# A two-layer diffusion trunk on 8 cores: first heads prepared in the projection, values two steps behind the scores, PSUM banks apart, 14 adaLN pieces moved into the feed-forward

## The chip, the cores and the metric

The program runs on all 8 cores of one Trainium2 chip (cores 0 to 3 are one die, 4 to 7 the other). Each core computes one share of the requests on its own, with no traffic between cores, and all of them read the same weights. The metric is the device time of the slowest core in microseconds. The engines of a core are TensorE (PE), ScalarE (ACT), VectorE (DVE), GpSimd (POOL) and SyncE (SP); POOL and SP also issue the DMAs.

## The reference, cut to what matters

```python
for i in range(2):                       # layer 0: pooling + latent attention, layer 1: gated MLP
    sh1, sc1, g1, sh2, sc2, g2 = split(silu(cond) @ ada_w[i] + ada_b[i], 6)      # adaLN, 6 x 1024
    h = rms_norm(x, norm_mix_g[i]) * (1 + sc1) + sh1
    if i == 0:
        z = h @ ab_w_in                  # u (512) | cq (384) | ckv (256) | krope (32)
        y_pool = (windowed_mean(u, w in (2, 4, 8, 16)) - u) @ w_pool * scale
        q = rope(rms_norm(rms_norm(cq) @ w_uq))          # 8 heads of 96
        k, v = rms_norm([rms_norm(ckv) @ w_ukv, krope]), ...   # 512 cached keys in front
        y = concat(y_pool, softmax(q k / sqrt(96)) v) @ ab_w_out
    else:
        y = chunk_gmlp(h)                # u * (W_s v + b), chunks of 128
    x = x + g1 * y
    h = rms_norm(x, norm_ffn_g[i]) * (1 + sc2) + sh2
    x = x + g2 * ((silu(h @ ffn_wg) * (h @ ffn_wu)) @ ffn_wd)          # D_FF 2816
```

Each core has 512 context tokens (2 sequences of 256) and 1024 latent tokens, which attend to 512 cached and the 1024 latent keys. Matmuls are bf16 with f32 sums.

## The kernel before, in words

The 1536 tokens are three blocks of 512 (block 0 is context). The residual `xb` stays in SBUF with features on the partitions. A helper class records every operation, so most instructions have the line of a helper (L230 is `mm`, L228 `mm` with a group check off, L239 a transpose, L247 an activation, L251, L259, L268 and L274 element-wise operations, L220 a DMA). Program order on each engine is the order in which the Python generators are stepped: a main generator yields, and fillers (other generators) are stepped between its pieces. The helper also makes every engine wait where two engines touch the same PSUM bank.

**Weights** come through one list (`ents`) in a fixed order, by one `Stream` of 11 slots of 512 KB (bf16; the f32 source is 1 MB). A slot's next DMA is issued on POOL's queue when `W.done` frees it. Slots 8, 9 and 10 are given up after their first use. All 48 adaLN pieces (`ada_piece`: 16 matmuls of 2 columns into one bank, then a small DVE addition into `mod`) come before the output projection's weights: 8 at the start, the others during the preparation of pair 0 and the attention.

**Stages of layer 0**, in order of time:

- `Norm.gen` squares a block (ACT, POOL), sums it on PE with a matrix of ones, and writes the normalised block `hy[b]`. Block 0 and the first 8 adaLN pieces go first.
- `inproj(b)` for b = 0, 1, 2: ten steps of 8 matmuls (kv, q, u and rotary parts), their norms and evacuations, in banks 0 to 5. While block b runs, the norm of block b + 1 is stepped (`weave_in`, by an account of estimated idle time), and with b = 1 also `pooling` of block 0. Block 2 has no filler.
- `qkv(0)` prepares keys, queries and values of the first pair of heads: 14 units (6 q, 4 k, 4 v), with smaller steps that are called one or more units later (`later`, `tick`): `reduce`, `rnorm`, `rotate`, `turn` (8 transposes), `sums`. Pooling of blocks 1 and 2 and some adaLN pieces are stepped beside it. Each pooling tile is made by narrow matmuls against `band`, evacuated by ACT (`pbf`), multiplied by `pool_w`, and evacuated again by ACT.
- `attention`: 4 pairs of heads, 28 steps each (4 context steps, 24 of one 128-key tile against 1024 queries). A step is `score` (2 matmuls of 512 columns into one of the two double banks `SD`, then one exp on ACT into `pt`), then `values` of the step before (8 matmuls of 65 columns, into banks 4 and 5). Between them `qkv` of the next pair, the adaLN pieces and `spread` (4 transposes) are stepped. All of these share banks 6 and 7 (`FB`) in turn.
- Output projection, then the feed-forward `ffn(0)`: groups of 3, 3, 3 and 2 weight pieces; `up` is 16 matmuls of 512 columns, `down` 6 (the last groups 10). Layer 1 follows (`gmlp`, `ffn(1)`).

The changed places are in `build`: the slots and `ents`, `ffn`, the code from `cached_keys` to the output projection.

Of the kernel before, what the change touches and what calls it, by code (L numbers as in the profile page):

```python
# [363 lines left out]
def build():  # L364
# [42 lines left out]
    with ExitStack() as es:  # L407
# [16 lines left out]
        slots = [new("wslot%d" % i, [128, 2048], BF16, high=(i >= 8)) for i in range(11)]  # L424
# [31 lines left out]
        ent_ada(8, 48)  # L456
# [31 lines left out]
        W.retire.update((8, 9, 10))  # L488
# [150 lines left out]
        def ffn(l, need):  # L639
# [37 lines left out]
            for gi in range(1, 4):  # L677
                for j in range(2 * (FGRP[gi][1] - FGRP[gi][0])):
# [3 lines left out]
                    if j % 2 == 1:  # L682
                        up_done(FGRP[gi][0] + j // 2)
# [144 lines left out]

        def inproj(b):
# [43 lines left out]
            if b == 0:  # L873
# [4 lines left out]
                held.append(ckvf)  # L878
            pq.append(proj(5, W.get("in_q1"), 0))
# [30 lines left out]
        FB = (6, 7)  # L910

        def pooling(blocks, banks, step, evac):

            for b in blocks:
                seqs = [(0, 2), (2, 4)] if b == 0 else [(4, 12)]
                for g in range(4):
# [22 lines left out]
                    evac(pbf[:], ps[:], 1.0 / w)  # L939
# [31 lines left out]
        for b in range(3):  # L971
            drain(norms[b])
            fill = collections.deque()
            if b < 2:
                fill.append(norms[b + 1])
            if b > 0:
                fill.append(pooling([b - 1] if b == 1 else [], (6,), 1.3, lambda o, i, sc: P.ts("dve", o, i, sc, None, ALU.mult)))
            weave_in(inproj(b), fill)
        for key in ("in_kv", "in_q0", "in_q1", "in_u0", "in_u1"):
            W.done(key)  # L980
        N.close()
        drop(*sqb.t, *rsb.t, *t2k.t, sqkr, ropek, *held)

        wukv = W.get("ukv")
        wuq = [W.get("uq0")[:, 0, :], W.get("uq0")[:, 1, :], W.get("uq1")[:, 0, :]]
        ptr = Ring([new("pt%d" % i, [128, 1024], BF16) for i in range(3)])
        rdr = Ring([new("rd%d" % i, [128, 4], F32) for i in range(2)])

# [6 lines left out]
        kvq = [new_kvq(0)]  # L995
        qfr = Ring([new("qf%d" % i, [128, 4, 96], F32) for i in range(5)])
        qsr = Ring([new("qs%d" % i, [128, 4, 96], F32) for i in range(2)])
        qtr = Ring([new("qt%d" % i, [128, 4, 96], BF16) for i in range(6)])
        qrr = Ring([new("qr%d" % i, [128, 2, 4, 32], F32) for i in range(2)])
        sqk = Ring([new("sqk%d" % i, [128, 512], BF16) for i in range(2)])  # L1000
        ssr = Ring([new("ss%d" % i, [128, 8], F32) for i in range(4)])

        def qkv(p, banks):
# [3 lines left out]
            for hl in range(2):  # L1007
                P.dma("sp", kT[64:96, hl, :], kro[64:96, :], "kro%d" % (p % 2))
# [16 lines left out]
            def turn(b, qts):  # L1025
                ps = P.bank(banks).bitcast(BF16)
# [28 lines left out]
            def q_unit(b, u):  # L1055
# [3 lines left out]
                ps = P.bank(banks)  # L1059
# [7 lines left out]
                P.cp("dve", qf[:].rearrange("p a d -> p (a d)"), ps[:, 0:384])  # L1067
# [10 lines left out]
            def sums(kb, sq):  # L1078
                ps = P.bank(banks)
# [5 lines left out]
            def k_unit(kb):  # L1085
                ps = P.bank(banks)
# [7 lines left out]
            def v_unit(kb):  # L1094
                ps = P.bank(banks)
# [3 lines left out]
                P.cp("dve", V[:, kb * 4:kb * 4 + 4, :, 0:64], ps[:].rearrange("p (t h d) -> p t h d", t=4, h=2))  # L1099
# [7 lines left out]
            order = [("q", b, u) for b in range(3) for u in range(2)] + [(c, kb) for kb in (3, 0, 1, 2) for c in "kv"] if p == 0 else [("q", 0, 0), ("k", 3), ("q", 0, 1), ("v", 3), ("q", 1, 0), ("k", 0), ("q", 1, 1), ("v", 0),  # L1107
# [28 lines left out]
        def spread(p, ytok, b):  # L1136
            ps = P.bank(FB).bitcast(BF16)
# [260 lines left out]
```

How the kernel before makes its waits and increments, by code:

```python
    def op(self, e, fn, reads, writes, inc=True):  # L181
        rr = [x for x in (self.reg(a) for a in reads) if x is not None]
        wr = [x for x in (self.reg(a) for a in writes) if x is not None]
        waits = self._waits(e, self._deps(rr, wr, e))
        eng = self.E[e]
        attach = (e != "pe")
        for s, v in (waits[:-1] if attach else waits):
            eng.wait_ge(self.sem[s], v)
        ins = fn(eng)
        if waits and attach:
            ins._wait_ge(self.sem[waits[-1][0]], waits[-1][1])
        if inc:
            ins.then_inc(self.sem["c_" + e], 1)
            self.cnt[e] += 1
            ev = ("c_" + e, self.cnt[e])
        else:
            ev = ("c_" + e, self.cnt[e] + 1)
        self._record(rr, wr, ev)
        self.nins += 1
        return ins
# [1 line left out]
    def dma(self, q, out, in_, key, slow=False):  # L202
        rr = [x for x in (self.reg(in_),) if x is not None]
        wr = [x for x in (self.reg(out),) if x is not None]
        waits = self._waits(q, self._deps(rr, wr))
        eng = self.E[q]
        for s, v in waits:
            eng.wait_ge(self.sem[s], v)
        k = self.dsem(key)
        side = out if wr else in_
        nm = side.tensor.name
        last = self.dlast.get(k)
        if last is not None and last != nm and self.known[q].get(k, 0) < self.dtot[k]:
            eng.wait_ge(self.sem[k], self.dtot[k])
            self.known[q][k] = self.dtot[k]
        self.dlast[k] = nm
        if slow:
```

## Time and profile before

| | us |
|---|---|
| median of 3 runs (lowest, highest) | 1257.72 (1257.38, 1264.88) |
| profiled execution, its own time | 1258.27 |
| span of its slowest core, core 2 | 1257.2 |
| spans of the 8 cores | 1245.5 to 1257.2 |
| PE, DVE, ACT, POOL busy | 1130.3, 478.0, 428.9, 226.9 |

### The profile page before, as it was taken

How to read it: one execution, taken by the hardware profiler on the slowest of the kernel's cores; microseconds unless marked ns; L12 is line 12 of the kernel's file. 1: busy time of each engine (PE TensorE's matmuls, PEld its weight loads, DVE VectorE, ACT ScalarE, POOL GpSimd, SP SyncE). 2: the span in 40 equal slices, each digit the busy share in tenths (PEclk: the TensorE clock that was granted, in tenths of full speed). 3: DMA queues.
4: the chain of work that ended last, by engine and by line, in shares of the span. 5: the costliest groups of instructions: out<-in, count | busy, mean ns of one | idle time of the engine just before them, and what ended most of it. 6: DMA issues, size and time to landing. Idle time of an engine off the chain costs nothing.

```text
span 1257.2 us, 17850 instructions; the slowest of 8 cores (1245.5 to 1257.2 us)
## 1 busy us (share of the span) xinstructions
PE 1130.3 (90%) x6857; PEld 547.4 (44%) x6857; DVE 478.0 (38%) x814; ACT 428.9 (34%) x669; POOL 226.9 (18%) x347
## 2 busy tenths in 40 slices
PE   2447877887899999999999999998899999999998
PEld 1223455555443444444444444443344444444443
DVE  0335445555136311151251263565522215125133
ACT  2435457777735511101101156543541110110100
POOL 4311245335113100000000022234310000000000
PEclk9988879899699999999999999998899999999999
DMA  9980245775991434215225206004534421400013
GB/s 189 229 152 1 43 73 93 127 130 100 162 168 21 64 56 78 34 34 84 34 34 84 51 1 109 1 1 63 92 48 68 67 36 32 84 17 1 1 78 124
DMA packets 24977, 90.04 MB, mean 72 GB/s; under 512 B 3392, under 2 KB 3776, under 8 KB 24128
## 3 DMA queue, kind: packets, MB, share of 16 engines
q0 software_dynamic: 21312, 77.10, 36.7%
q1 hardware_dynamic: 3584, 11.80, 2.8%
q8 instruction: 58, 0.95, 0.3%
q14 instruction: 23, 0.19, 0.1%
HBM read 153.85 MB, written 6.88 MB: 128 GB/s over the span
## 4 chain that ended last, share of the span: by engine, by line
PE 76%; DMA 6%; DVE 5%; ACT 5%; issue 4%; POOL 3%; POOLq 0%; ACTq 0%; DVEq 0%
PE pb L230 74%; DMA band<-band 3%; ACT pt L247 3%; DMA wslot<-ada_w 3%; PE pb L228 2%; DVE xtmp L268 1%; DVE kT L274 1%; POOL wslot L220 1%; PE pb L239 1%; POOL qs L251 1%; DVE xb L268 0%; POOL xtmp L251 0%; ACT hy L247 0%; POOL xsq L251 0%; DVE ytk L251 0%
## 5 line engine op out<-in xcount | busy, mean ns | idle before, releaser
L230 PE MATMUL pb<-hb,wslotx 128*128 128x512 bf16 x1200 | 264.5, 379 | 0.0
L230 PE MATMUL pb<-hb,wslot 128*128 128x512 bf16 x1104 | 247.8, 384 | 0.0
L247 ACT ACTIVATE sg<-pb 128x512 f32<-128x512 f32 x132 | 78.7, 596 | 472.7 <-PE pb L230 472.7
L251 DVE TENSOR_TENSOR apart<-pb,sg 128x512 bf16<-128x512 f32 x132 | 91.3, 692 | 369.1 <-PE pb L230 346.2
L268 DVE SCALAR_TENSOR_TENSOR xb<-pb,mod,xb 128x512 f32<-128x512 f32 x192 | 143.7, 749 | 146.1 <-PE pb L230 146.1
L230 PEld LDWEIGHTS pb<-hb,wslotx 128*128 128x128 bf16 x1200 | 117.4, 98 | 141.6
L230 PEld LDWEIGHTS pb<-hb,wslot 128*128 128x128 bf16 x1104 | 109.0, 99 | 133.3 <-issue 6.0
L230 PE MATMUL pb<-apart,wslot 128*128 128x512 bf16 x768 | 167.1, 379 | 0.0
L247 ACT ACTIVATE pt<-pb,rk 128x1024 bf16<-128x1024 f32 (+1 forms) x128 | 117.8, 952 | 42.3 <-PE pb L230 41.4
L230 PEld LDWEIGHTS pb<-apart,wslot 128*128 128x128 bf16 x768 | 75.2, 98 | 90.2
L230 PE MATMUL pb<-hy,wslot 128*128 128x512 bf16 (+1 forms) x336 | 84.5, 404 | 6.6 <-ACT hy L247 4.5
L230 PE MATMUL pb<-qT,kT 96*128 96x512 bf16 (+1 forms) x224 | 73.8, 417 | 0.0
L268 DVE SCALAR_TENSOR_TENSOR xtmp<-xb,AA,xrs 128x512 f32<-128x512 f32 x72 | 62.5, 906 | 9.8 <-ACT xrs L247 9.4
L247 ACT ACTIVATE xsq<-xb 128x512 bf16<-128x512 f32 x72 | 41.9, 622 | 67.6 <-PE pb L230 36.3
L230 PE MATMUL pb<-apart,wslotx 128*128 128x512 bf16 x288 | 62.5, 379 | 0.0
L228 PEld LDWEIGHTS pb<-V,pt 128*128 128x128 bf16 x768 | 36.1, 103 | 56.9 <-issue 49.7
L230 PE MATMUL pb<-xsq,ones 128*128 128x512 bf16 x96 | 30.2, 409 | 31.3 <-ACT xsq L247 23.7
L228 PE MATMUL pb<-V,pt 128*128 128x65 bf16 x768 | 43.4, 203 | 16.1 <-ACT pt L247 15.0
L230 PEld LDWEIGHTS pb<-hy,wslot 128*128 128x128 bf16 (+1 forms) x336 | 34.1, 103 | 52.2 <-issue 19.2
L251 POOL TENSOR_TENSOR xtmp<-xb,xrs 128x512 f32<-128x512 f32 x24 | 33.7, 1403 | 117.6 <-ACT hb L247 86.4
L247 ACT ACTIVATE hb<-xtmp,mod 128x512 bf16<-128x512 f32 x54 | 37.6, 720 | 33.5 <-DVE xtmp L268 33.5
L230 PE MATMUL pb<-uTb,wslot 128*128 128x512 bf16 x192 | 47.4, 401 | 0.0
(131 smaller groups left out, 936.2 us busy)
## 6 DMA issues: line engine op xcount, KB each, us to landing
wslot<-ada_w POOLq DMA_DIRECT2D x48, 512.0 KB, 7.3
wslot<-ffn_wd POOLq DMA_DIRECT2D x16, 512.0 KB, 10.4
wslot<-ffn_wu POOLq DMA_DIRECT2D x12, 512.0 KB, 7.8
wslotx<-ffn_wg POOLq DMA_DIRECT2D x12, 512.0 KB, 16.9
y<-xb SPq DMA_DIRECT2D x12, 512.0 KB, 2.6
wslot<-ffn_wg POOLq DMA_DIRECT2D x10, 512.0 KB, 7.4
wslotx<-ffn_wu POOLq DMA_DIRECT2D x10, 512.0 KB, 15.4
xb<-x_in POOLq DMA_DIRECT2D x4, 1024.0 KB, 44.5
```

The source lines that it names most:

```text
L220: ins = eng.dma_start(out=out, in_=in_)
L228: return self.op("pe", lambda g: g.matmul(out, lhsT, rhs, start=start, stop=stop, skip_group_check=True), [lhsT, rhs], [out], inc=inc)
L230: return self.op("pe", lambda g: g.matmul(out, lhsT, rhs, start=start, stop=stop), [lhsT, rhs], [out], inc=inc)
L239: return self.op("pe", lambda g: g.transpose(out, in_, ident), [in_, ident], [out])
L247: return self.op("act", lambda g: g.activation(out=out, in_=in_, func=func, bias=bias, scale=scale), reads, [out])
L251: return self.op(e, lambda g: g.tensor_tensor(out=out, in0=in0, in1=in1, op=op), [in0, in1], [out])
L268: return self.op(e, lambda g: g.scalar_tensor_tensor(out=out, in0=in0, scalar=sc, in1=in1, op0=op0, op1=op1), reads, [out])
L274: return self.op(e, lambda g: g.tensor_copy(out=out, in_=in_), [in_], [out])
```

## The change

1. The stream has 10 slots in place of 11, and slots 7, 8 and 9 are given up after their first use; an eighth slot (`wsloty`) comes back at the start of attention, and 8 in place of 7 behind it.
2. 14 adaLN pieces (34 to 47) leave the list before the output projection and stand among the weights of `ffn(0)`, two behind each of the up pieces 3 to 9. Each pair is computed when the up piece is done. `ensure_AA` of layer 1's second norm moves behind `ffn(0)`.
3. The cached keys' squares (`cached_keys`) move from ahead of `inproj(0)` into it.
4. `together` steps the fillers of `inproj` evenly: all of the norm of block 1 in block 0, all of the norm of block 2 with pooling of block 0 in block 1, and 12 steps of `qkv(0)` in block 2, in banks 6 and 7. The order of units of `qkv(0)` is new, and its q and v evacuations go to ACT. The rest of `qkv(0)` then runs beside pooling of blocks 1 and 2, whose evacuations alternate between ACT and DVE and whose product comes one tile later, with four banks each.
5. In attention `values` runs two steps behind `score`. The large tiles of `qkv` have bank 6 alone; its small tiles, `spread` and the adaLN pieces have bank 7 alone.
6. The rotary keys are copied into each of the two key buffers once, not once for each pair.

```diff
-        slots = [new("wslot%d" % i, [128, 2048], BF16, high=(i >= 8)) for i in range(11)]
+        slots = [new("wslot%d" % i, [128, 2048], BF16, high=(i >= 7)) for i in range(10)]
...
                     ent(("wu", l, k), ffn_wu[l, k], 8, 256)
+                    if l == 0 and 3 <= k < 10:
+                        ent_ada(34 + 2 * (k - 3), 36 + 2 * (k - 3))
...
-        ent_ada(8, 48)
+        ent_ada(8, 34)
...
-                        up_done(FGRP[gi][0] + j // 2)
+                        k = FGRP[gi][0] + j // 2
+                        up_done(k)
+                        if l == 0 and 3 <= k < 10:
+                            for _ in range(2):
+                                ada_piece(pool=B7)
...
-                    evac(hy[b][:, g, :], ps2[:], vecs[:, 128 + g:129 + g])
-                    yield step
+                    late.append((b, g, pbf))
+                    if len(late) > lag:
+                        product(*late.popleft())
+                        yield step
...
+        drain(norms[0])
+        together(inproj(0), 10, [(norms[1], 26)])
+        drain(norms[1])
+        pool0 = pooling([0], (6,), 1.3, (on_dve, on_dve))
+        together(inproj(1), 10, [(norms[2], 36), (pool0, 9)])
...
+        bk0 = [FB]
+        q0 = qkv(0, bk0, bk0)
+        together(inproj(2), 10, [(q0, 12)])
...
-                    if pend is not None:
-                        for b in values(*pend):
-                            todo.append((i + 2, functools.partial(spread, pend[0], pend[3], b)))
+                    if len(pend) == 2:
+                        sums(pend.popleft())
...
-                    pend = (p, step, pt, ytok)
+                    pend.append((p, step, pt, ytok))
...
-        together(qkv(0, (0, 1, 2, 3, 4, 5)), 18, [(pool12, 18), (ada, 6)])
+        together(pooling([1, 2], (4, 5, 6, 7), 0.5, (in_turn, in_turn), 1), 16, [(q0, 9)])
+        drain(q0)
...
-            nxt[0] = qkv(p + 1, FB) if p < 3 else iter(())
+            nxt[0] = qkv(p + 1, [(6,)], [SB]) if p < 3 else iter(())
```

**POOL's queue ahead of `band`.** Before (`cckv` and `band` are inputs of the cached values and of pooling; `w_ukv`, `w_uq` and `ada_w` are weights):

```order
L220 DMA wslot_16_58<-w_ukv 128x2048
L220 DMA wslot_17_59<-w_uq 128x1536
L220 DMA wslot_18_60<-w_uq 128x768
L220 DMA wslot_19_61<-ada_w 128x2048
L220 DMA wslot_20_62<-ada_w 128x2048
L220 DMA wslot_21_63<-ada_w 128x2048
L251 TENSOR_TENSOR xtmp_48_123<-xb_1_43,xrs_46_121 128x512
L251 TENSOR_TENSOR xtmp_49_124<-xb_1_43,xrs_46_121 128x512
L220 DMA ckvn_35_99<-cckv 128x1024
L220 DMA band_89<-band 128x1728
```

Now:

```order
L220 DMA wslot_17_59<-w_ukv 128x2048
L220 DMA wslot_18_60<-w_uq 128x1536
L220 DMA wslot_19_61<-w_uq 128x768
L220 DMA wslot_20_62<-ada_w 128x2048
L251 TENSOR_TENSOR xtmp_47_121<-xb_1_43,xrs_45_119 128x512
L251 TENSOR_TENSOR xtmp_48_122<-xb_1_43,xrs_45_119 128x512
L220 DMA ckvn_34_97<-cckv 128x1024
L220 DMA band_87<-band 128x1728
```

One adaLN piece stands ahead of `band` where three stood; the rest of the list ahead of it has the same bytes.

**PE in the second block of the attention's first pair.** Before (`qT,kT` is a score, `V,pt` the values, `cqn` a q unit, `ckvn` on the left a k unit):

```order
L230 MATMUL pb<-qT_82_1005,kT_81_1004 128x512 x2
L228 MATMUL pb<-V_83_1006,pt_76_999 128x65 x8
L230 MATMUL pb<-qT_82_1005,kT_81_1004 128x512 x2
L228 MATMUL pb<-V_83_1006,pt_77_1000 128x65 x8
L230 MATMUL pb<-ckvn_32_96,wslot_16_58 128x512 x2
L230 MATMUL pb<-scT_55,wslot_21_63 128x2 x16
L230 MATMUL pb<-qT_82_1005,kT_81_1004 128x512 x2
L228 MATMUL pb<-V_83_1006,pt_78_1001 128x65 x8
L230 MATMUL pb<-wslot_17_59,cqn_95 128x192 x2
```

Now:

```order
L230 MATMUL pb<-qT_72_849,kT_71_848 128x512 x2
L228 MATMUL pb<-V_73_850,pt_101_1219 128x65 x8
L230 MATMUL pb<-ckvn_31_94,wslot_17_59 128x512 x2
L230 MATMUL pb<-qT_72_849,kT_71_848 128x512 x2
L228 MATMUL pb<-V_73_850,pt_102_1220 128x65 x8
L230 MATMUL pb<-wslot_18_60,cqn_93 128x192 x2
```

The rows of a step look alike; the `pt` that the values read is now that of two scores earlier. The q unit behind a k unit still comes one step later, and here the k unit has no adaLN piece behind it.

**PE at the start of `inproj(2)`.** Before:

```order
L230 MATMUL pb<-hy_40_104,wslot_22_64 128x512 x16
L230 MATMUL pb<-hy_40_104,wslot_23_65 128x512 x8
L230 MATMUL pb<-sqb_53_128,ones_47 128x512
L230 MATMUL pb<-sqb_54_129,ones_47 128x512
L230 MATMUL pb<-hy_40_104,wslot_23_65 128x512 x8
```

Now:

```order
L230 MATMUL pb<-hy_39_102,wslot_22_64 128x512 x8
L230 MATMUL pb<-wslot_18_60,cqn_93 128x192 x2
L230 MATMUL pb<-wslot_19_61,cqn_93 128x192
L230 MATMUL pb<-wslot_18_60,cqn_93 128x192 x2
L230 MATMUL pb<-wslot_19_61,cqn_93 128x192
L230 MATMUL pb<-hy_39_102,wslot_22_64 128x512 x8
L230 MATMUL pb<-wslot_18_60,cqn_93 128x192 x2
L230 MATMUL pb<-wslot_19_61,cqn_93 128x192
```

The groups of 8 now have units of `qkv(0)` between them. In `ffn(0)` two runs of 16 two-column matmuls (`scT`) stand behind the sixth up tile pair of each piece, with nothing else moved there.

## Rows read from the trace of the kernel before

**Rows 1.** Spans and clock: the slowest core and the fastest.

```profile
core 2: 1257.2 us, clock 0.955
core 4: 1245.5 us, clock 0.971
```

**Rows 2.** Busy time by stretch: stretch, length, each engine busy (instructions), clock, DMA.

```profile
core 2: us, PE busy (x) PEld busy (x) DVE busy (x) ACT busy (x) POOL busy (x), PEclk, DMA share, GB/s
79.00:90.00 11.00, 0.56 (x6) 0.59 (x7) 0.04 (x1) 0.00 (x0) 0.00 (x0) 0.65 0.93 140
90.00:123.00 33.00, 26.76 (x129) 11.33 (x126) 20.29 (x43) 17.72 (x29) 4.05 (x3) 0.86 0.00 0
123.00:144.00 21.00, 20.47 (x102) 9.49 (x102) 7.22 (x11) 8.91 (x16) 0.92 (x2) 0.91 0.00 1
144.00:180.00 36.00, 22.57 (x267) 17.46 (x266) 18.29 (x49) 16.93 (x34) 17.47 (x36) 0.73 0.49 89
180.00:226.00 46.00, 38.54 (x520) 25.62 (x521) 23.14 (x55) 33.19 (x45) 19.38 (x39) 0.83 0.57 92
226.00:272.00 46.00, 38.16 (x570) 25.60 (x571) 26.44 (x66) 34.47 (x48) 19.85 (x40) 0.93 0.67 118
272.00:317.00 45.00, 35.27 (x547) 24.10 (x544) 24.82 (x59) 32.28 (x42) 20.57 (x41) 0.96 0.68 118
317.00:354.00 37.00, 32.10 (x370) 17.11 (x368) 5.66 (x23) 28.82 (x30) 7.39 (x14) 0.72 1.03 162
500.00:600.00 100.00, 100.00 (x465) 45.36 (x464) 31.85 (x44) 11.94 (x20) 4.75 (x9) 1.00 0.30 50
```

**Rows 3.** Timeline, 36 to 90 us: start, duration, instruction, idle before it.

```profile
36.46 0.56 PE L230 MATMUL pb<-scT,wslot 128*128 128x2 bf16 x16 [3.02 <-DMA wslot<-ada_w]
39.64 0.51 PEld L230 LDWEIGHTS pb<-scT,wslot 128*128 128x128 bf16 x16 [2.70 <-issue]
39.67 0.56 PE L230 MATMUL pb<-scT,wslot 128*128 128x2 bf16 x16 [2.65 <-DMA wslot<-ada_w]
47.62 0.54 POOL L220 DMA_DIRECT2D band<-band  x1
89.44 1.02 PE L228 MATMUL pb<-band,utok 128*128 128x129 bf16 x8 [12.22 <-DMA band<-band]
90.25 3.06 PE L230 MATMUL pb<-hy,wslot 128*128 128x512 bf16 x8
93.36 1.89 PE L230 MATMUL pb<-hy,wslot 128*128 128x512 bf16 x8
```

**Rows 4.** PE's timeline, 116 to 126 us: the first groups of block 2.

```profile
117.68 1.91 PE L230 MATMUL pb<-hy,wslot 128*128 128x512 bf16 x3 [3.29 <-ACT hy L247]
120.23 2.42 PE L230 MATMUL pb<-hy,wslot 128*128 128x512 bf16 x4 [0.63 <-ACT hy L247]
123.22 3.14 PE L230 MATMUL pb<-hy,wslot 128*128 128x512 bf16 x7 [0.58 <-ACT hy L247]
```

**Rows 5.** What PE waited for, 145 to 190 us: total, times, longest.

```profile
PE pb L230 <- DVE pbf L251: 4.8, 3, 1.8
PE pb L239 <- POOL qt L251: 4.2, 3, 2.5
PE pb L230 <- DVE mod L251: 2.4, 2, 1.7
```

**Rows 6.** What PE waited for, 190 to 352 us.

```profile
PE pb L228 <- ACT pt L247: 14.0, 35, 0.7
PE pb L230 <- DVE kT L274: 5.7, 8, 1.1
```

**Rows 7.** Groups of PE, 190 to 352 us: busy, mean ns, idle before.

```profile
L230 PE MATMUL pb<-scT,wslot 128*128 128x2 bf16 x528 | 18.6, 164 | 5.1 <-DVE kT L274 2.1 <-DVE qT L259 0.9 <-DVE V L274 0.8
```

**Rows 8.** Timeline around one k unit, 228 to 236 us.

```profile
229.87 1.06 PE L230 MATMUL pb<-ckvn,wslot 128*128 128x512 bf16 x2
230.96 0.60 ACT L247 ACTIVATE sqk<-pb 128x512 bf16<-128x512 f32 x1 [0.60 <-PE pb L230]
231.59 1.41 DVE L274 CAST kT<-pb 64x512 bf16<-64x512 f32 x2 [0.48 <-PE pb L230]
```

**Rows 9.** ACT's timeline in the last pair, 329 to 354 us.

```profile
330.96 1.11 ACT L247 ACTIVATE pt<-pb,rk 128x1024 bf16<-128x1024 f32 x1 [0.61 <-PE pb L230]
335.48 1.11 ACT L247 ACTIVATE pt<-pb,rk 128x1024 bf16<-128x1024 f32 x1 [0.61 <-PE pb L230]
342.02 10.98 ACT L247 ACTIVATE pt<-pb,rk 128x1024 bf16<-128x1024 f32 x10 [0.40 <-PE pb L230]
```

More of the change, by code:

```diff
@@ L878, in inproj @@
                 held.append(ckvf)
+            if b == 2:
+                W.done("in_kv")
+                W.done("in_q0")
             pq.append(proj(5, W.get("in_q1"), 0))
@@ L910, in build, with pooling, product @@
         FB = (6, 7)
-        def pooling(blocks, banks, step, evac):
+        SB = (7,)
+        def pooling(blocks, banks, step, evac, lag=0):
+            late = collections.deque()
+            def product(b, g, pbf):
+                ps2 = P.bank(banks)
+                P.mm(ps2[:], pw[:, g, :], pbf[:])
+                evac[1](hy[b][:, g, :], ps2[:], vecs[:, 128 + g:129 + g])
             for b in blocks:
@@ L954, in pooling @@
                     drop(*[utok.pop(t) for t in range(4, 12)])
+            while late:
+                product(*late.popleft())
+                yield step
         pbr = Ring([new("pbf%d" % i, [128, 512], BF16) for i in range(2)])
@@ L969, in weave_in @@
                     debt = 0.0
[L971 to L987, printed above, removed]
         def new_kvq(i):
@@ L993, in new_kvq, with rotary_keys, qkv @@
             return d
[L995 to L1003, printed above, removed]
+        def rotary_keys(p):
+            for hl in range(2):
+                P.dma("sp", kvq[p % 2]["kT"][64:96, hl, :], kro[64:96, :], "kro%d" % (p % 2))
+        def qkv(p, banks, small):
             d = kvq[p % 2]
             kT, qT, V, rk = d["kT"], d["qT"], d["V"], d["rk"]
-            for hl in range(2):
-                P.dma("sp", kT[64:96, hl, :], kro[64:96, :], "kro%d" % (p % 2))
+            if p == 1:
+                rotary_keys(p)
             lag = collections.deque()
@@ L1025, in turn @@
             def turn(b, qts):
-                ps = P.bank(banks).bitcast(BF16)
+                ps = P.bank(small[0]).bitcast(BF16)
                 for hl in range(2):
@@ L1058, in q_unit @@
                 ss, sr, qts = qst[b]
-                ps = P.bank(banks)
+                ps = P.bank(banks[0])
                 for i in range(2):
@@ L1078, in sums @@
             def sums(kb, sq):
-                ps = P.bank(banks)
+                ps = P.bank(small[0])
                 for i in range(4):
@@ L1085, in k_unit @@
             def k_unit(kb):
-                ps = P.bank(banks)
+                ps = P.bank(banks[0])
                 P.mmg(ps[:], [(wukv[:, kc, p * 256:p * 256 + 128], ckvn[kb][:, kc, :]) for kc in range(2)])
@@ L1094, in v_unit @@
             def v_unit(kb):
-                ps = P.bank(banks)
+                ps = P.bank(banks[0])
                 for i in range(4):
@@ L1187, in attention, with sums @@
             steps = [("ctx", hl, s) for hl in range(2) for s in range(2)] + [("lat", hl, n) for hl in range(2) for n in range(12)]
-            pend = None
+            pend = collections.deque()
             i = 0
             todo = collections.deque()
+            def sums(w):
+                for b in values(*w):
+                    todo.append((i + 2, functools.partial(spread, w[0], w[3], b)))
             for p in range(4):
@@ L1228, in before @@
             drain(nxt[0])
-            nxt[0] = qkv(p + 1, FB) if p < 3 else iter(())
-        left = 50 - ada_state["done"]
+            nxt[0] = qkv(p + 1, [(6,)], [SB]) if p < 3 else iter(())
+        left = 36 - ada_state["done"]
         for i, _ in enumerate(attention(before)):
@@ L1244, in build @@
             drop(*r.t)
-        drop(cqn, *ckvn, kro, krs, band, icnt, pw, ropeq, gqr)
+        drop(cqn, *ckvn, kro, krs, ropeq, gqr)
         hbs = [new("hb%d" % i, [128, 8, 512], BF16) for i in range(3)]
         N = Norm()
-        W.more([new("wslotx%d" % i, [128, 2048], BF16) for i in range(7)])
+        W.more([new("wslotx%d" % i, [128, 2048], BF16) for i in range(8)])
         norms = {}
```

92 lines of the change are left out of this document (61 added, 31 removed).

## The prediction, made before the changed kernel had run

> **What bounds the kernel now.** I read the table by stretch first. PE is fully busy through the feed-forward [rows 2], in its row of 500 to 600 us, so what is added there is paid in full, and what can be won lies ahead of 354 us, where PE idles. Then the timeline for the first stall: PE stands still for 12.22 us until `band` has landed, with POOL, ACT and DVE idle too [rows 2, 3]. Next the start of block 2, where PE waits 3.29, 0.63 and 0.58 us for normalised tiles [rows 4]. From 144 to 180 us, the preparation of pair 0, PE is busy 22.57 of 36 us at a clock of 0.73 [rows 2], and the waits name evacuations and rotations one by one [rows 5]: a chain of latencies, no full engine. In attention, 180 to 354 us, PE is busy 144.1 us and ACT 128.8 us of 174 [rows 2]; PE's largest wait is for the exps, 14.0 us in 35 pieces, then for the key copies, 5.7 us [rows 6].
>
> **The start and block 1.** PE's last two adaLN pieces of the start came 3.21 us apart (36.46 to 39.67), each after a wait for its DMA [rows 3]: that is the price of a piece on the full queue. Two fewer stand ahead of `band`, so it lands 6.4 us earlier, near 83. The bounds are 0 (another transfer is last) and 12.2 (the whole wait goes). Behind the stall, 8 matmuls take 3.06 us where the next 8 take 1.89 [rows 3]: 1.2 us of low clock, mostly gone with a wait of two or three us. One more projection group (1.9) and three sums of squares (3 x 0.2) now stand ahead of `band` and fill what is left of the wait: 2.5 us. With the norm of block 2 stepped evenly, it is done inside block 1, and the 4.5 us of rows 4 go. Sum 14.6. Against it: ACT and DVE are busy 17.7 and 20.3 of 33 us there [rows 2], and the norm's squares now stand in ACT's queue ahead of the projection's own; I charge 2.6 us. **Term: -12 us** (-4 to -16). Moving the cached keys costs nothing: ACT's 0.6 us and DVE's small work fall beside 8 matmuls.
>
> **Block 2 and pair 0.** From 123 to 178 us, 55 us, PE is busy 20.5 + 22.6 us [rows 2]. Of the latter, five adaLN pieces (5 x 0.56, the duration in rows 3) leave and the first scores (1 us) belong to attention; 18.7 us stay, at a clock of 0.73. If half of the low clock's time comes back, that is some 15.5, so PE's work is 36. Block 2 had 8.9 us of ACT and 7.2 of DVE in 21 [rows 2]; it can take half of `qkv(0)` and become 26 to 27 us long. The other half beside pooling has 16 evacuations of pooling, 8 each on ACT and DVE, and no longer waits for each one's product (4.8 us in rows 5), but the last rotation chain of POOL (4.2 us in rows 5) still ends before the last transposes. I put stalls at 5 us: 41 in place of 55. **Term: -14 us.** Bounds: -18 (almost no stall) and -5 (half the stall stays and the clock stays low).
>
> **Attention.** The values of a step now wait for an exp that is one step older, so the 14 us in 35 pieces [rows 6] go, and about 1 us of the same ahead of 190. The score two steps on waits for the same exp (its double bank), so no wait of the other kind is lost or gained. Nine adaLN pieces fewer (26 in place of 35), at 0.56 us: -5.0; the same price, 18.6 us for 33 pieces, stands in [rows 7]. Against it: a k unit holds its bank from the matmuls' start at 229.87 to the end of the key copies at 233.0, 3.1 us [rows 8], and with bank 6 alone the next large tile waits for all of it. By the calls (18 in 25 steps) two of four k units in a pair have the next tile one step, some 1.4 us, behind them: 6 x 1.4 = 8.4 us where 5.7 stood, +2.7. Small tiles collide in bank 7 in turn, transposes (an evacuation of 0.8 us) ahead of an adaLN piece above all, as they did in two banks. The last pair will be bound by the exps: the last ten came 1.10 us apart (10.98 us) [rows 9], so 24 of them and four context steps make some 30 us where 37 are now; 5 of these 7 us are waits counted above, so a further gain is left out. To be careful I leave +2 us for exps that PE now has to wait for where ACT is behind. 14 + 1 + 5 - 2.7 - 2 = 15.3. **Term: -15 us.** Bounds: -33 (the low clock in 180 to 354, 0.83, 0.93, 0.96 and 0.72 in rows 2, goes as well) and +3 (every k unit stalls PE and the exps' wait moves to the scores).
>
> **Feed-forward.** 14 pieces of 0.56 us on a full PE: **+7.8 us.** The 16 weight loads of a piece took 0.51 us [rows 3], so they lie within the 0.56. The Trainium skill ("TensorE: Matmul & The Clock Gate", LDWEIGHTS) gives a load as its columns divided by 1.2 GHz, 107 ns for 128, which would make a piece 1.7 us, the term 24 and the total 1241; the row is at 32 ns, between the two figures of its section on weight-path modes for a fast load (32 cycles, and half of 107 ns). The DMAs are hidden: the queue's share is 0.30 there [rows 2], and each pair of pieces stands far ahead of its use. The rotary copies left out and the slots cost nothing: SP has little else, and the output projection's stretch waits for no weight.
>
> **Sum**, against the profiled execution's own 1258.27, which is 0.5 us above the median: -12 - 14 - 15 + 7.8 = -33. **Predicted 1225 us.**
>
> **The rivals.**
>
> *The wait is exchanged.* The exps' wait ends, but scores, k units in bank 6 and small tiles in bank 7 take its place: the k unit's 3.1 us against a step of 1.5 speaks for it, that PE and ACT are both under 83% busy speaks against. Attention gains only its five us for the pieces: 1225 + 10 = 1235, and with less gained in block 2, 1240. Chance 0.24, with the case that the values' lag does nothing, because PE already queues behind the score's own wait.
>
> *The clock comes back.* In rows 2 the clock is 0.73 to 0.96 from 90 to 354 us; the slowest core has 0.955 over the span, the fastest 0.971, and the two differ by 11.7 us [rows 1]. If fewer stalls hold PE at 2.4 GHz, the last pair alone gains 4 to 5 us: steps there take 4.52 us for three (330.96 to 335.48), where the last ten took 1.10 each [rows 9]. With as much in the pairs before and in 144 to 180: 1225 - 15 = 1210. For it: idle time falls. Against it: PE did little in the steps at low clock that it won't do again. The same page of the Trainium skill (The HAM clock gate) says that activity releases the throttle and idling restores it, which is this rival; the rows agree after the 12 us wait. Chance 0.18.
>
> *The feed-forward starves.* The 14 pieces share slots and queue with its weights, and stand ahead of the down weights in a list that keeps its order. If the queue were full there, each would cost its 3.2 us: 14 x 3.2 = 45, and 1225 + 45 = 1270, slower than before. It decides only from a share near 1; the row has 0.30, and 45 us over the 200 us of pieces 3 to 9 add 0.22. Chance 0.05.
>
> *The preparation doesn't fit into block 2* (ACT's queue holds back the projection's squares, POOL's chain ends as late as before): term -5 and block 1's -4 give 1225 + 17 = 1242. Chance 0.08.
>
> **How the numbers follow.** The forecast has 0.45, with 1215 to 1236 as its own range. For 8 in 10 the range takes in the clock's case and the exchanged wait: 1203 to 1244. This kernel's time can be told apart within about 1%, 12.6 us. Faster than 1245 are the forecast, the clock, most of the exchanged wait and most of the last case: 0.84; within 1%: 0.10; slower by over 1%: 0.06.
>
> **What would show it.** `band`'s wait under 4 us and its matmuls near 83 us; no wait for `hy` at block 2's start; the first score near 152 us; PE's wait for `pt` under 3 us and that for `kT` near 8; attention some 161 us long where it is 176; 14 runs of `scT` in the feed-forward at 0.56 us each, with no DMA wait. I am wrong if attention is as long as now with another name in its wait list, or if the first score comes after 165 us.

## The result, and the profile after

The changed kernel takes 1240.77 us (median of 3 runs, 1240.61 to 1241.51) where the kernel before takes 1257.72: a ratio of 0.9858, 95% interval 0.9808 to 0.9907. It is 17 us faster, where 33 had been forecast. Executions in which one die was granted a lower clock throughout are left out of every ratio in this document. 1240.8 lies inside the range of 1203 to 1244, but outside the forecast's own 1215 to 1236, and next to the rival "the wait is exchanged" (1235 to 1240).

The spans of all cores fell. The slowest is now core 6; core 4, the fastest before [rows 1], fell by 7 us only. Both lines are of the changed kernel's list of cores:

```profile
core 2: 1231.4 us, clock 0.977
core 6: 1240.5 us, clock 0.972
```

Busy time by stretch of core 6 after the change, with the columns of [rows 2], cut at its own stages: block 1 behind `band`, block 2, the rest of pair 0's preparation, the four pairs of attention, the feed-forward.

```profile
83.00:109.00 26.00, 19.77 (x113) 9.29 (x115) 16.79 (x39) 14.90 (x25) 3.58 (x4) 1.00 0.01 1
109.00:135.00 26.00, 23.98 (x157) 12.70 (x156) 13.29 (x26) 15.59 (x31) 6.94 (x13) 1.00 0.00 1
135.00:158.00 23.00, 14.12 (x138) 11.37 (x139) 13.87 (x32) 9.38 (x19) 9.71 (x23) 0.78 0.64 92
158.00:203.00 45.00, 33.73 (x477) 24.30 (x478) 23.38 (x54) 31.69 (x44) 17.42 (x35) 0.92 0.35 61
203.00:252.00 49.00, 38.99 (x500) 28.11 (x504) 24.60 (x59) 32.74 (x45) 18.18 (x37) 0.83 0.44 71
252.00:297.00 45.00, 33.99 (x471) 25.25 (x476) 24.53 (x58) 30.43 (x42) 18.74 (x38) 0.89 0.44 76
297.00:336.00 39.00, 30.23 (x414) 19.49 (x412) 7.45 (x27) 31.02 (x36) 8.99 (x17) 0.93 1.01 161
500.00:600.00 100.00, 99.45 (x541) 46.60 (x548) 32.14 (x50) 11.34 (x19) 7.93 (x15) 1.00 0.49 88
```

Set beside [rows 2], the stretches ahead of attention shrank and those of attention did not: on this core the pairs take 45, 49, 45 and 39 us where they took 46, 46, 45 and 37. PE is busy less in them (137 us against 144), so its idle time grew. The feed-forward's DMA share went from 0.30 to 0.49 with PE at 99% busy.

The start, on PE's timeline (start, duration, instruction, idle before it). It answers to [rows 3]:

```profile
82.12 0.84 PE L230 MATMUL pb<-xsq,ones 128*128 128x512 bf16 x3
82.91 0.61 PE L228 MATMUL pb<-band,utok 128*128 128x129 bf16 x8
83.36 1.89 PE L230 MATMUL pb<-hy,wslot 128*128 128x512 bf16 x8
```

`band`'s matmuls come at 82.91 in place of 89.44 and wait for nothing (on the other cores 0.8 to 3.2 us); the group behind them takes 1.89 us where it took 3.06. Block 2's first matmul starts at 108.94 and the group waits for no tile. Before [rows 4] it started at 117.68 and got its last normalised tile at 123.22, with seven matmuls of block 2 done by then.

What PE waited for between block 2 and the first score, 134 to 158 us (total, times, longest), where [rows 5] stood:

```profile
PE pb L239 <- POOL qt L251: 3.7, 3, 1.8
PE pb L239 <- DVE ksb L251: 3.1, 1, 3.1
PE pb L230 <- ACT hy L247: 1.0, 2, 0.7
PE pb L230 <- DVE pbf L251: 0.8, 1, 0.8
```

And in attention, 158 to 335 us, in answer to [rows 6]:

```profile
PE pb L230 <- DVE kT L274: 11.9, 10, 2.1
PE pb L228 <- DVE rd L1174: 6.6, 4, 2.6
PE pb L230 <- ACT pt L247: 6.0, 20, 0.9
PE pb L239 <- DVE rd L1174: 2.4, 2, 1.7
PE pb L239 <- DVE hy L274: 2.3, 2, 2.1
PE pb L230 <- DVE qT L259: 1.3, 2, 1.0
```

The values no longer wait for exps (L228 on `pt` is down to 0.8 us). The scores now do: by the means over the cores they wait 4.5 us for exps, where they waited for none before. Beside that PE waits for DVE: for key copies, twice as long as before, for the reciprocals (`rd`) that empty the values' banks between two heads, and for small tiles. One k unit, on the timeline of all engines, answers to [rows 8]:

```profile
169.64 0.38 PE L230 MATMUL pb<-ckvn,wslot 128*128 128x512 bf16 x1
170.39 0.59 ACT L247 ACTIVATE sqk<-pb 128x512 bf16<-128x512 f32 x1
171.01 1.41 DVE L274 CAST kT<-pb 64x512 bf16<-64x512 f32 x2 [1.13 <-ACT sqk L247]
172.57 0.66 PE L230 MATMUL pb<-wslot,cqn 128*128 128x192 bf16 x6 [1.87 <-DVE kT L274]
```

The square stands behind an exp on ACT, the two copies behind the square on DVE, and the q unit one step later waits 1.87 us for the bank. Every score behind it in PE's queue waits too. In the last pair ACT sets the pace, as [rows 9] did in its last ten exps: here twelve in 12.58 us.

```profile
320.06 12.58 ACT L247 ACTIVATE pt<-pb,rk 128x1024 bf16<-128x1024 f32 x12 [0.18 <-PE pb L230]
```

To compare kernels I cut each core's PE timeline at three marks (first score, first matmul of the output projection, end) and took means over the 8 cores of the profiled execution. Waits, busy time and granted clock of PE are between the first two marks, in attention; the waits are listed by what they waited for. All waits and the busy time add up to the stretch within 1.2 us:

| kernel | ratio to before | first score at | attention | behind it | waits: pt | kT | rd | all | busy | clock |
|---|---|---|---|---|---|---|---|---|---|---|
| before | 1 | 177.9 | 175.2 | 899.4 | 17.6 | 6.7 | 1.9 | 32.3 | 142.0 | 0.90 |
| after | 0.9858 | 158.3 | 172.7 | 903.8 | 5.6 | 11.2 | 9.1 | 37.4 | 134.9 | 0.90 |
| lag2_only | 0.9980 | 179.5 | 172.1 | 897.9 | 6.6 | 10.9 | 7.6 | 31.4 | 140.2 | 0.88 |
| lag1 | 0.9872 | 160.5 | 173.6 | 904.7 | 19.1 | 9.3 | 1.6 | 38.3 | 134.8 | 0.93 |
| shared | 0.9823 | 159.5 | 167.6 | 903.2 | 5.4 | 9.7 | 8.1 | 32.2 | 135.1 | 0.89 |
| ada_back | 0.9910 | 160.0 | 184.7 | 897.8 | 4.4 | 10.3 | 8.5 | 37.5 | 146.9 | 0.85 |
| slots10 | 0.9968 | 174.2 | 174.5 | 898.3 | 18.5 | 6.7 | 1.9 | 33.9 | 139.9 | 0.91 |
| prep_only | 0.9851 | 160.2 | 174.9 | 897.5 | 17.5 | 5.2 | 1.0 | 28.8 | 144.9 | 0.89 |
| spaced | 0.9715 | 159.8 | 155.6 | 903.4 | 5.7 | 6.4 | 1.4 | 25.5 | 129.6 | 0.92 |
| ada21 | 0.9764 | 159.6 | 160.3 | 906.7 | 6.7 | 7.9 | 8.9 | 30.9 | 129.2 | 0.92 |
| sp_lag1 | 0.9818 | 160.9 | 170.4 | 903.7 | 19.9 | 0.2 | 1.5 | 32.4 | 137.6 | 0.89 |
| sp_bank | 0.9744 | 160.5 | 159.3 | 904.1 | 6.3 | 9.3 | 1.4 | 29.5 | 128.9 | 0.94 |
| sp_eleven | 0.9713 | 159.5 | 156.2 | 903.7 | 5.6 | 6.7 | 1.4 | 25.6 | 130.0 | 0.92 |
| sp_ada21 | 0.9703 | 161.1 | 152.0 | 907.0 | 7.2 | 6.8 | 1.6 | 26.1 | 125.4 | 0.94 |

So the change's 17.8 us of mean span are -19.6 ahead of attention, -2.5 in it and +4.3 behind it.

### The profile page after: what moved, and what is told of

Same layout as the page of the kernel before. It is cut to its first block, busy times and chain, and to the rows that moved or that the text cites. A ratio compares the mean times of both kernels' runs of the same rounds, so it can differ in the third digit from the quotient of the medians.

```text
span 1240.5 us, 17691 instructions; the slowest of 8 cores (1231.4 to 1240.5 us)
## 1 busy us (share of the span) xinstructions
PE 1114.8 (90%) x6753; PEld 552.4 (45%) x6857; DVE 476.9 (38%) x812; ACT 424.0 (34%) x671; POOL 225.4 (18%) x347
## 4 chain that ended last, share of the span: by engine, by line
PE 76%; DVE 7%; ACT 6%; issue 5%; POOL 4%; DMA 3%; DVEq 0%; POOLq 0%; ACTq 0%
PE pb L230 74%; ACT pt L247 3%; DMA wslot<-ada_w 3%; DVE xtmp L268 2%; PE pb L228 1%; DVE kT L274 1%; POOL qr L251 1%; DVE xb L268 1%; ACT hy L247 1%; PE pb L239 1%; POOL wslot L220 1%; POOL qt L251 1%; POOL qs L251 0%; ACT xsq L247 0%; ACT hb L247 0%
## 5 line engine op out<-in xcount | busy, mean ns | idle before, releaser
L230 PE MATMUL pb<-hb,wslot 128*128 128x512 bf16 x1031 | 239.4, 381 | 1.4
L230 PE MATMUL pb<-hb,wslotx 128*128 128x512 bf16 x1037 | 233.8, 379 | 1.1
L230 PEld LDWEIGHTS pb<-hb,wslot 128*128 128x128 bf16 x1056 | 103.5, 98 | 125.1 <-issue 2.3
L230 PEld LDWEIGHTS pb<-hb,wslotx 128*128 128x128 bf16 x1056 | 103.0, 98 | 123.8
L230 PE MATMUL pb<-apart,wslotx 128*128 128x512 bf16 x566 | 135.5, 379 | 0.5
L230 PE MATMUL pb<-apart,wslot 128*128 128x512 bf16 x468 | 114.1, 379 | 0.7
L230 PEld LDWEIGHTS pb<-apart,wslotx 128*128 128x128 bf16 x576 | 56.4, 98 | 67.5
L230 PE MATMUL pb<-hy,wslot 128*128 128x512 bf16 (+1 forms) x281 | 72.8, 405 | 7.5 <-ACT hy L247 4.4
L230 PEld LDWEIGHTS pb<-apart,wslot 128*128 128x128 bf16 x480 | 46.8, 98 | 56.2
L228 PEld LDWEIGHTS pb<-V,pt 128*128 128x128 bf16 x768 | 40.4, 104 | 36.6 <-issue 20.4
L228 PE MATMUL pb<-V,pt 128*128 128x65 bf16 x768 | 44.0, 203 | 8.7 <-DVE rd L1174 6.6
L247 ACT ACTIVATE hb<-xtmp,mod 128x512 bf16<-128x512 f32 x54 | 37.5, 720 | 33.4 <-DVE xtmp L268 33.4
L230 PEld LDWEIGHTS pb<-hy,wslot 128*128 128x128 bf16 (+1 forms) x288 | 29.1, 103 | 44.3 <-issue 17.2
## 6 DMA issues: line engine op xcount, KB each, us to landing
wslot<-ffn_wg POOLq DMA_DIRECT2D x12, 512.0 KB, 11.6
wslotx<-ffn_wg POOLq DMA_DIRECT2D x9, 512.0 KB, 12.5
```

The costliest lines, as they stand in the source:

```text
L228: return self.op("pe", lambda g: g.matmul(out, lhsT, rhs, start=start, stop=stop, skip_group_check=True), [lhsT, rhs], [out], inc=inc)
L230: return self.op("pe", lambda g: g.matmul(out, lhsT, rhs, start=start, stop=stop), [lhsT, rhs], [out], inc=inc)
L247: return self.op("act", lambda g: g.activation(out=out, in_=in_, func=func, bias=bias, scale=scale), reads, [out])
```

## The experiments

The theory after the result: in attention PE takes its work in order, and the waits that it meets on DVE are a queue behind the exps' wait; taking that one away lets PE arrive earlier at the next. The rival is the prediction's sum: each part is worth its price, and some other part lost the rest. Each ratio is to the kernel before, run on the same chip beside it. The twelve kernels fall into three groups, each with a chip of its own: lag2_only, lag1, shared and ada_back; spaced, ada21, slots10 and prep_only; the four named sp_. Between groups a stage can shift without any edit: `band`'s first matmul is at 89.7 us before and at 91.6 in lag2_only, which has the same start.

**lag2_only**: the kernel before with the values two steps behind.

```diff
-                    if pend is not None:
-                        for b in values(*pend):
...
+                    if len(pend) == 2:
+                        sums(pend.popleft())
...
```

> The kernel before, with one part of the change alone: the values run two steps behind the scores. If the prediction's term holds, the 14 to 15 us of waits for exps in attention go and nothing takes their place: 1257.7 - 14 = 1244, with PE's wait for pt under 3 us. If the rival holds (the wait is exchanged), PE now queues at the scores, at the bank of a k unit and at the values' banks behind DVE: 1252 to 1258, with waits for kT, rd and pt at the scores that together grow by 8 us or more.

Measured: 0.9980 (0.9966 to 0.9994), 2.5 us. PE's waits of its slowest core, 190 to 352 us:

```profile
PE pb L230 <- DVE kT L274: 7.6, 7, 2.0
PE pb L228 <- DVE rd L1133: 6.6, 3, 2.3
PE pb L230 <- ACT pt L247: 4.7, 16, 0.5
PE pb L239 <- DVE kT L274: 3.1, 2, 1.9
PE pb L230 <- DMA wslot<-ada_w: 2.9, 3, 1.7
```

By the means, `pt` falls from 17.6 to 6.6 us (the values' part from 17.6 to 0.8, while the scores' part rises from nothing to 5.7), `kT` and `rd` rise by 9.9, and all waits together stay at 31 to 32. That is the exchange, shown with one edit. The prediction's 14 us are refuted for this order of work.

**lag1**: the changed kernel with the values one step behind.

```diff
-                    if len(pend) == 2:
+                    if len(pend) == 1:
```

> The changed kernel with the values one step behind the scores again, everything else kept. Prediction's term: 1240.8 + 14 = 1255. Rival: 1241 to 1246, and PE's waits for kT and rd shrink by about what the wait for pt grows.

Measured: 0.9872 (0.9854 to 0.9891) where the changed kernel has 0.9858. That is 1.8 us, the intervals overlap, and attention is 0.9 us longer by the means. Again `pt` is up by 13.5 and `kT` and `rd` down by 9.4. The prediction's 1255 is out.

**shared**: the changed kernel with banks 6 and 7 in turn for all tiles.

```diff
-        SB = (7,)
+        SB = FB
-            nxt[0] = qkv(p + 1, [(6,)], [SB]) if p < 3 else iter(())
+            nxt[0] = qkv(p + 1, [FB], [FB]) if p < 3 else iter(())
```

> The changed kernel with banks 6 and 7 shared in turn by all tiles of attention again, as before the change. In the changed kernel PE waits 11.9 us for kT where it waited 5.7 before. If bank 6 alone is what doubled it, the wait falls back to about 6 and the time to 1233 to 1236. The prediction's price for the banks was 2.7 us: 1238. If the waits belong to PE's order and not to the banks, the time stays within 1240 to 1242.

Measured: 0.9823 (0.9804 to 0.9842), attention 5.1 us shorter by the means. The two ratios' intervals overlap, but all of the 5.1 us is waits (37.4 to 32.2 in the table), so I take the split to cost 4 to 5 us, more than the 2.7 predicted. What stands behind a wait can't be read from its releaser alone: `kT` fell by 1.5 only, because in shared banks small tiles wait for key copies too. Sorted by what waits, the large tiles (k, q and v units) wait 14.6 us in the changed kernel and 5.6 here, by the means; the small ones (transposes, `spread`, adaLN pieces) 8.8 and 12.0. So the cost is in bank 6, where the prediction had it, and the small tiles lost less with a bank of their own. The q units, changed kernel first, then `shared`, on the slowest core of each (columns as in [rows 7]):

```profile
L230 PE MATMUL pb<-wslot,cqn 128*128 128x192 bf16 x108 | 13.0, 261 | 10.2 <-DVE kT L274 9.2 <-DVE V L274 0.8
L230 PE MATMUL pb<-wslot,cqn 128*128 128x192 bf16 x108 | 13.1, 263 | 4.5 <-DVE kT L274 3.1 <-DVE hy L274 0.6 <-DVE V L274 0.4
```

**ada_back**: the changed kernel with the 14 pieces back in attention.

```diff
-                    if l == 0 and 3 <= k < 10:
-                        ent_ada(34 + 2 * (k - 3), 36 + 2 * (k - 3))
...
-        ent_ada(8, 34)
+        ent_ada(8, 48)
```

> The changed kernel with the 14 adaLN pieces back in attention, none in the feed-forward. The prediction's prices: the feed-forward wins 7.8 us, attention loses 9 to 14 pieces at 0.56: 5 to 8 us, so 1238 to 1241. If attention is held by waits in which the pieces had found cover, it loses under 3 us: 1234 to 1236, and moving them had been a loss.

Measured: 0.9910 (0.9889 to 0.9932). Both expectations had it at 1241 or faster; it is 6 us slower than the changed kernel. The feed-forward wins 6 us, attention loses 12: 0.86 us a piece against 0.43. Moving the pieces paid 6 us, where the prediction's one price of 0.56 us, in either place, made it even. The adaLN pieces' own waits rose from 3.1 to 10.4 us, but all waits together stayed (37.4 and 37.5): the 12 us are busy time, 134.9 to 146.9, of which 14 pieces at 0.40 to 0.56 us explain 6 to 8. The rest goes with a granted clock of 0.85 in place of 0.90.

**slots10**: the kernel before with the new slots alone.

```diff
-        slots = [new("wslot%d" % i, [128, 2048], BF16, high=(i >= 8)) for i in range(11)]
+        slots = [new("wslot%d" % i, [128, 2048], BF16, high=(i >= 7)) for i in range(10)]
...
-        W.retire.update((8, 9, 10))
+        W.retire.update((7, 8, 9))
...
-            if k == 1:
+            if k == 2:
...
+        W.more([new("wsloty", [128, 2048], BF16)])
```

> The kernel before with the stream's 10 slots alone (7 to 9 given up, the eighth back in attention): two adaLN pieces fewer ahead of band. If band alone decides the start of block 1, its first matmul comes 6 us earlier, near 83 us, and the time falls by 5 to 6 us, to 1252. If the time is lost again before attention, because the norm of block 2 isn't ready, it falls by under 2 us.

Measured: 0.9968 (0.9951 to 0.9984), 4 us. `band`'s first matmul comes at 85.2 in place of 89.7 by the means, with a wait of 5.9 us ahead of it in place of 11.7. The line of the slowest core:

```profile
85.57 1.02 PE L228 MATMUL pb<-band,utok 128*128 128x129 bf16 x8 [4.79 <-DMA band<-band]
```

The first score comes 3.7 us earlier: what the queue gives is kept.

**prep_only**: the changed kernel with values one step behind, shared banks and all pieces in attention (the edits of lag1, shared and ada_back together).

> The changed kernel with the values one step behind, banks 6 and 7 shared and all adaLN pieces in attention: what is left is the start, the even stepping and pair 0's preparation in block 2. By the stages measured so far the first score comes 20 us earlier than before the change, and attention carries 5 pieces more than before (34 in place of 35 and 5 outside it, now 40): 1257.7 - 20 + 4 = 1242, 0.987. If attention loses more than that because it starts with less done, 1247 or more.

Measured: 0.9851 (0.9831 to 0.9872), where the whole change has 0.9858. The start and the preparation carry all of the gain that can be told. The three parts that touch attention are worth nothing measurable together, with five more pieces in attention at that.

**spaced**: `shared`, with the 18 calls of the next pair's preparation at chosen steps: a free step behind each k unit, none where a head's values end.

```diff
-            n = i % 28
-            for k in range((n + 1) * 18 // 25 - n * 18 // 25):
-                next(nxt[0], None)
+            if i % 28 in (2, 3, 5, 6, 7, 8, 10, 11, 12, 13, 15, 18, 19, 21, 22, 23, 24, 25):
+                next(nxt[0], None)
```

(The k units fall on steps 3, 8, 13 and 19 of 28, and nothing more is called in 4, 9, 14 and 20.)

> The changed kernel with banks 6 and 7 shared (it measured 0.9823 of the kernel before), and the 18 calls of the next pair's preparation at other steps: behind each k unit a step without a call, and none at the steps where a head's values end. If single long stalls behind a k unit and behind the values' evacuation are what attention loses, PE's waits for kT and rd, 9.7 and 8.1 us, fall by 10 us in sum and the time falls by 6 to 9 us, to 0.976. If waits are only exchanged again (the exps and the low clock bound attention), the wait for pt grows by as much and the time stays at 0.982.

Measured: 0.9715 (0.9691 to 0.9739), 13.6 us below `shared`, with attention at 155.6 us. PE's waits of its slowest core, 159 to 315 us:

```profile
PE pb L230 <- DVE kT L274: 6.6, 9, 0.9
PE pb L239 <- POOL qt L251: 5.9, 3, 2.5
PE pb L230 <- ACT pt L247: 4.4, 17, 0.7
PE pb L230 <- DVE V L274: 1.9, 4, 0.6
PE pb L230 <- DVE rd L1174: 0.9, 3, 0.5
```

In `shared`, on its slowest core from 159 to 327 us, the first two stood so:

```profile
PE pb L228 <- DVE rd L1174: 7.0, 3, 2.6
PE pb L230 <- DVE kT L274: 6.7, 7, 1.6
```

By the means `rd` falls from 8.1 to 1.4, `kT` from 9.7 to 6.4, in pieces of 0.9 us at most where the longest had 1.9, and `pt` grows by 0.3 only; the waits of transposes for POOL's rotations (`qt`) grow from 3.0 to 5.8. The run moves two things at once, and it doesn't separate them: twice as much went from `rd` (no call where a head's values end) as from `kT` (a free step behind a k unit). All waits fell by 6.7 us, of 12.0 us that attention lost; the rest is PE's busy time, 135.1 to 129.6, with the clock up from 0.89 to 0.92.

**sp_lag1**: `spaced` with the values one step behind (the edit of lag1).

> The kernel of the run 'spaced' (0.9715 of the kernel before) with the values one step behind the scores again. With the long DVE stalls gone, the two theories of the lag part: if the lag had been worth nothing because other waits took its place, it should now be worth its 12 us of exp waits, and this run comes out at 0.981. If the lag is worth little in itself, since ACT and PE take turns as the limit, it stays at 0.972 to 0.974.

Measured: 0.9818 (0.9798 to 0.9837). Here the lag is worth 13 us, and attention is 14.8 us longer without it: the size of the prediction's -14, in another schedule. It isn't the prediction's 14 us of waits, though. `pt` is up by 14.2, but all waits by 6.9 only; the other 8.0 us are busy time, 129.6 to 137.6, with the clock down from 0.92 to 0.89. Its slowest core, 159 to 327 us:

```profile
PE pb L228 <- ACT pt L247: 16.4, 34, 1.1
PE pb L228 <- DVE ytk L251: 4.0, 5, 0.8
PE pb L239 <- POOL qt L251: 2.9, 3, 1.7
```

**sp_bank**: `spaced` with the split banks of the change (the edit of shared, undone).

> The kernel of the run 'spaced' with large tiles in bank 6 alone and small ones in bank 7 alone, as in the change. If the split costs because the next large tile comes one step behind a k unit, the free step now covers it and the split costs nothing or less: 0.970 to 0.972. If small tiles colliding in bank 7 (transposes, adaLN pieces, the spread) are the cost, it stays near the 5 us that it costs in the changed kernel: 0.975.

Measured: 0.9744 (0.9727 to 0.9761); attention is 3.6 us longer. The intervals overlap, but the waits say the same as in `shared`: those of the large tiles rise from 6.7 to 11.3 us, those of the small ones fall from 11.6 to 10.4.

**ada21**: `shared` with 21 pieces in the feed-forward, three behind each of the up pieces 3 to 9.

```diff
-                        ent_ada(34 + 2 * (k - 3), 36 + 2 * (k - 3))
+                        ent_ada(27 + 3 * (k - 3), 30 + 3 * (k - 3))
...
-                            for _ in range(2):
+                            for _ in range(3):
```

> The changed kernel with banks shared, and 21 adaLN pieces in the feed-forward in place of 14 (three behind each of the up pieces 3 to 9). By the prediction's prices a piece costs 0.56 us in either place: no change, 0.982. By the run with the 14 pieces put back, where attention grew by 12 us, a piece costs 0.86 there against 0.56: 7 more moved give 2 us, 0.9805.

Measured: 0.9764 (0.9748 to 0.9780), 7.4 us below `shared` by the ratios. By the means of the two profiled executions attention is 7.3 us shorter and the stretch behind it 3.5 longer, 3.7 us in all. The two kernels are of different groups, and the runs don't say which figure is nearer. By the means a piece cost 1.0 us in attention, 0.5 in the feed-forward; of the 7.3 us, 1.3 are waits and 5.9 busy time, at a clock of 0.92 in place of 0.89.

**sp_ada21**: the edits of spaced and ada21 together.

> The two edits that won by themselves, together: the calls spaced (0.9715) and 21 adaLN pieces in the feed-forward (0.9764, 7 us out of attention for 3.5 us there, against 0.9823 with shared banks alone). If their gains are apart, 0.966. If the spaced calls already took the waits that a piece caused, a piece costs 0.56 us in either place and it stays at 0.971.

Measured: 0.9703 (0.9681 to 0.9724), with `spaced` at 0.9715: no difference that can be told. Attention is 3.6 us shorter for 7 pieces, 0.5 each, and the stretch behind it as much longer. So with spaced calls a piece costs the same in either place. Both beat the kernel before and the changed one; sp_ada21's median is 1223.27 us and that of `spaced` 1223.20.

**sp_eleven**: `spaced` with one call fewer in block 2.

```diff
-        together(inproj(2), 10, [(q0, 12)])
+        together(inproj(2), 10, [(q0, 11)])
```

> The kernel of the run 'spaced' with 11 in place of 12 calls of pair 0's preparation in block 2, so that the transposes of block 1's queries leave banks 6 and 7 and come when banks 0 to 3 are free, and those of block 2 come behind the last pooling tile. In the changed kernel PE waits 3.1 us for bank 7 behind block 2, and 2.8 us for the last rotations. If these waits are what the preparation's term missed, the first score comes 3 to 5 us earlier: 0.968. If the chain of POOL and the low clock set the first score, it does not move: 0.9715.

Measured: 0.9713 (0.9694 to 0.9732), first score at 159.5 against 159.8. The waits of this stretch changed places and nothing was won: 134 to 160 us, slowest core,

```profile
PE pb L230 <- DVE ksb L251: 2.1, 1, 2.1
PE pb L239 <- POOL qt L251: 1.7, 1, 1.7
PE pb L230 <- DVE pbf L259: 1.2, 1, 1.2
PE pb L230 <- ACT V L273: 0.8, 1, 0.8
```

## Why the prediction was right and wrong, by its steps

- **The start and block 1, -12 us: right, with two of its parts off.** `band` at 82.9 (forecast 83), the waits for `hy` gone. Block 2 starts 8.7 us earlier (117.68 to 108.94) and no longer loses 4.0 us between its first matmul and 123.22 (5.54 us for seven matmuls of 0.22): -12.7 in all. The price of 3.2 us a piece on the full queue fits: slots10 takes 5.9 us of 6.4 off the wait for `band`, and 4.5 off its time. The crowding did show, and was more than the 2.6 us charged: PE's idle time in block 1, the wait for block 2's tiles left out, went from 1.7 us (89.5 to 117.68) to 6.2 (83 to 109). Low clock was undercounted on the other side: 0.92 over that stretch before, 1.00 now, where I had counted one group.
- **Block 2 and pair 0, -14 us: the direction right, the size not.** From block 2's first matmul to the first score it is 48.9 us. Before it was 54.9 from 123.22 on, with 1.5 us of block 2 already done, so -6 by the prediction's own cut and -7.5 like for like. Block 2 took 26.4 us, as forecast. Behind it I had 14 us and it was 22.5. The term that was mis-sized is the 5 us of stalls for both parts together: PE is idle 2.0 us in block 2 and 8.9 behind it. Its work was 38.1 us where I had 36, with the clock at 0.78 behind block 2. sp_eleven moved the calls of the largest wait (3.1 us, transposes in bank 7 behind `ksb`), and a wait of 2.1 us for `ksb` took its place with no gain, so moving them is not enough. What sets this stretch (POOL's rotations, DVE's queue behind block 2, the clock) stays open.
- **Attention, -15 us: this failed; it gave 2.5.** The step that failed is "the 14 us in 35 pieces go", with its only charges 2.7 for key copies and 2 for exps. The values' wait for exps went, as said (17.6 to 0.8 us by the means). "No wait of the other kind is lost or gained" was wrong: the scores' wait for the same exps went from nothing to 4.5. `rd`, which has no term in the sum, rose by 7.2, and `kT` by 4.5. I had priced what would take the wait's place from waits measured while PE still came late to DVE's results. All waits together rose by 5.1 us; attention is shorter at all because PE's busy time fell by 7.1, of which nine pieces at 0.40 to 0.56 us explain 4 to 5. lag2_only shows the exchange alone; `spaced` beside sp_lag1 shows that the lag gives 13 us in another schedule, about half of it in waits. The rival that says this had been written down at 0.24, and the prediction's own sign of being wrong, attention as long as now with another name in its wait list, is what came. The total fell inside the wide range because that range had been made to hold this rival, not because the sum was right.
- **Bank 6 alone, +2.7 us: the sign and the mechanism right, the size low.** The large tiles' waits are 9.0 us longer than with shared banks, the small tiles' 3.2 shorter. The product of the sum was also off by its own rows: a bank held for 3.1 us that is wanted again 1.4 us later costs the remaining 1.7, so six such cases make 10.2, not 8.4.
- **Nine pieces at 0.56 us: too low.** A piece in that attention cost 0.86 to 1.0 us by ada_back and ada21, nearly all of it PE's busy time at a lower granted clock. Why the clock was lower there isn't shown.
- **Feed-forward, +7.8 us: somewhat high.** By the means it is +4.3 against before and about +6 between kernels that differ in this (897.5 and 897.8 against 903.2 to 904.7). The row's 0.56 us is longer than what a run keeps PE from the next instruction: on the timeline that one starts 0.40 us after the run's start.

```profile
206.88 0.54 PE L230 MATMUL pb<-scT,wslot 128*128 128x2 bf16 x16
207.28 0.38 PE L230 MATMUL pb<-qT,kT 96*128 96x256 bf16 x2
```

  The 24 us that the Trainium skill's plain formula for a weight load ("TensorE: Matmul & The Clock Gate", LDWEIGHTS) would have made of it is ruled out by these rows: a load with its matmul took 25 ns. The 32 cycles that the prediction quotes beside it stand on that page for fp8, and the weights here are bf16.
- **The starving feed-forward: excluded.** The share went to 0.49 (0.52 had been worked out), with no wait for a weight.
- **The clock's return: partly.** The slowest core has 0.972 in place of 0.955. Between block 2's start and the first score it went from 0.81 (123 to 178 us) to 0.90 (109 to 158); in attention the mean of the cores stays at 0.90.

The sum was 33.2 us and the mean span fell by 17.8. Ahead of attention 26 us had been forecast and 19.6 came, a miss of 6.4; attention missed by 12.5; the feed-forward gives 3.5 back.

## What to carry to other kernels

When a wait on an engine that works in order is taken away, don't book its length: ask which result it will reach for next, and how long that result's own engine is behind at that moment; waits measured before the edit were shortened by the one that you remove. Place fillers before adding lag or banks: none on the steps where the main work's own banks are emptied, and a free step behind one whose evacuation takes longer than a step (here 3.1 us against 1.4). The same lag was worth 2 us with crowded calls and 13 with spaced ones; which of the two rules gave more was not tried alone. Sort waits by what waits as well as by what they wait for: the two views of `shared` point to different banks. And take a short run's price from start to start on the timeline, and from a run with and without it, because its cost depends on what it queues behind.

## What the runs showed of the hardware that I had not expected

- A run of 16 two-column matmuls with 16 weight loads occupies PE for 0.40 us (206.88 to 207.28), 25 ns each, though the view lists 0.54 to 0.56 us of busy time.
- With shorter stalls the same work took less time: between `shared` and `spaced` PE's instructions are the same, and its busy time in attention is 5.5 us less at a granted clock of 0.92 in place of 0.89. With 14 more pieces (ada_back) the clock there was 0.85. It doesn't simply follow the sum of the waits: lag1 has the longest sum (38.3 us) and 0.93. What the clock followed in each case isn't settled by these runs.
